# Two norms in one chain, the gain of a norm moved beside its squares, and five changes of order, in a two-part transformer on one core

## The chip, the cores and the metric

One core of one Trainium2 chip runs the whole program in one launch. Time is device microseconds, the median of the runs. The engines are PE (TensorE; PEld is its weight load), DVE (VectorE), ACT (ScalarE), POOL (GpSimd) and SP (SyncE, which issues the weight DMAs here). L12 is line 12 of the kernel.

## The reference, cut to what matters

The model has width 1024 and 256 tokens x; 256 context tokens go beside them. Its first half has two layers of modulated norm, mixing (latent attention, Fourier and a long convolution), modulated norm, and an MLP with squared ReLU; it ends in a norm of x. The second half has a delta-rule layer and a gated linear attention (GLA) layer, each with an MLP, and takes its own context tokens.

```python
def rms_norm(x, g):
    y = x * rsqrt(mean(x * x) + 1e-6)
    return y * g

def modulate(h, shift, scale):
    return h * (1 + scale) + shift

# every norm inside the layers
h = modulate(rms_norm(x, g), shift, scale)
# end of the first half, start of the second
x = rms_norm(x, final_norm_g)
hx = modulate(rms_norm(x, norm_mix_g[0]), shift, scale)
hc = modulate(rms_norm(ctx, norm_mix_g[0]), shift_c, scale_c)
```

## The kernel before

The residual stream X is a tile of 128 partitions by 8 blocks of 128 features by 512 columns: 256 tokens x, then 256 of the context. Stages in which only x matters (the second layer's front, out and mlp, the GLA's out and the last mlp) work on 256 columns. Every product with a weight is three TensorE products in fp32r: high by high, high by rest, rest by high (L558, L559, L560), of which the rest is what the first rounding left. Weights come in slabs of 128 by 2048 through a ring of four, which SP fills in order. For each slab ACT writes w_high and DVE then w_rest. A slab is 48 matmuls.

The stages in order: mod, in0, up0, attention, front, out0, mlp0, norm, in1, up1, attention, front, out1, mlp1, final, conv, delta, read, out of the delta layer, mlp2, norm, gin, gla, out, mlp3. Each engine's instructions are written out by hand in functions named pe_, act_, dve_ and pool_ plus the stage; nothing reorders them. A `View` counts each semaphore through tables of uses (U_IN, U_MLP and so on).

A norm is made like this. In the stage before it, a block of the product is added to X (dve_residual, L1517), ACT squares the block (act_square, L473), DVE adds the squares up (dve_add_square, L479). PE sums over features with a matrix of ones (pe_sums, L493), ACT takes the root (L517), DVE the reciprocal (L521), and PE spreads it over partitions (pe_factors, L501). The head of the next stage then makes h in four steps for each of the eight blocks: dve_scale (X by the factor, L526), act_move (gain and shift, L532), a copy to the high part on ACT, and the rest on DVE:

```python
nc.vector.tensor_tensor(H, X, factors(T), ALU.mult)
nc.scalar.activation(H, H, ACT.Identity, bias=shift, scale=gain)
nc.scalar.activation(high, H, ACT.Copy)
nc.vector.tensor_tensor(rest, H, high, ALU.subtract)
```

At the seam of the halves (dve_final, act_final, pe_final) this is done twice: a norm of x that is written back to X (L1190), then squares, sums and root over X and the context; ACT then issues the DMA that spills X, and the convolution stage begins with a memset (L1813) and its head.

In the up stage queries and keys are made head by head; `weights(2)` makes the parts of the next slab. The delta stage begins with `meet`, at which all engines wait for each other; POOL then makes gates (L2351) and copies keys (L2359) for two units, and PE's first products over keys are L1986. In the GLA recurrence there are 16 units (direction, tile, head). For each, ACT takes exponentials of 128 by 1024 (L2887, two instructions), DVE scales queries by them (L2945), POOL keys (L3029), PE forms pair products in PSUM, and DVE copies eight masked blocks of them to ATG (L2960), of which block n holds pairs that lie in the n-th level of a triangle. PE then forms the outputs.

## Time and profile before

| | |
| --- | --- |
| median of 3 runs | 2904.25 us (2902.1 to 2904.61) |
| the profiled execution | 2905.02 us, its span 2902.9 us |
| PE, PEld busy | 94%, 78% |
| DVE, ACT, POOL busy | 57%, 41%, 13% |
| DMA | 343.36 MB, mean 118 GB/s |

The span runs from the first to the last instruction. The shares are averages over stages with different limits; what a stage waits for is read from its own rows.

### The profile page before, as it was taken

The numbers are of one execution on the slowest core, as the hardware profiler recorded it, in microseconds if no ns is written. First come the engines' busy times: TensorE is split into PE (matmuls) and PEld (weight loads), VectorE is DVE, ScalarE is ACT, GpSimd is POOL, SyncE is SP. The second block draws the span as 40 slices with busy tenths as digits, with TensorE's granted clock in tenths as the row PEclk, the third lists the DMA queues.
The fourth block names the chain that finished last, engine by engine and source line by source line (L and its number), as shares of the span: only waits on it lengthen the run. The fifth ranks groups of instructions, "written<-read, shape, count | busy, mean of one in ns | idle before, by whom it ended". The sixth has DMA issues, their size and how long they took to land.

```text
span 2902.9 us, 43802 instructions
## 1 busy us (share of the span) xinstructions
PE 2729.6 (94%) x16708; PEld 2265.2 (78%) x16708; DVE 1647.1 (57%) x2847; ACT 1177.6 (41%) x2145; POOL 370.2 (13%) x583
## 2 busy tenths in 40 slices
PE   6999899998898997999999999999999998988899
PEld 4756777777757996887688888877777787977899
DVE  4565533334665666885377777773433345468565
ACT  4343422223534445346344455552422234343443
POOL 0000000000000000000066666640000000023000
PEclk9999999999999998999999999999999999999999
DMA  7263244442363553223200000032444433210453
GB/s 281 87 248 130 88 188 159 173 160 86 121 229 132 177 185 144 89 102 109 94 1 1 1 1 1 1 117 87 152 172 170 171 116 127 73 59 15 150 184 144
DMA packets 49614, 343.36 MB, mean 118 GB/s; under 512 B 5296, under 2 KB 7344, under 8 KB 9776
## 3 DMA queue, kind: packets, MB, share of 16 engines
q1 hardware_dynamic: 44960, 324.03, 30.1%
q10 hardware_dynamic: 4496, 17.15, 1.5%
q8 instruction: 108, 1.77, 0.2%
q14 instruction: 50, 0.41, 0.1%
HBM read 333.82 MB, written 7.34 MB: 118 GB/s over the span
## 4 chain that ended last, share of the span: by engine, by line
PE 85%; DVE 8%; ACT 4%; issue 2%; DMA 2%; POOL 0%; DVEq 0%; ACTq 0%; SPq 0%; PEldq 0%; PEld 0%; POOLq 0%
PE ps L558 20%; PE ps L560 20%; PE ps L559 20%; PE ps L2030 4%; PE ps L2017 3%; PE ps L764 3%; PE ps L2009 2%; PE ps L2038 2%; DMA ring<-in_w_dram 2%; PE ps L819 1%; DVE ring_rest L546 1%; ACT H L532 1%; PE ps L1986 1%; PE ps L1972 1%; PE ps L794 1%
## 5 line engine op out<-in xcount | busy, mean ns | idle before, releaser
L558 PE MATMUL ps<-hidden_high,w_high 128*128 128x256 f32 (+1 forms) x1160 | 389.2, 336 | 8.9 <-DVE h_rest L554 6.1
L1130 ACT ACTIVATE w_high<-ring 128x2048 fp32r<-128x2048 f32 x124 | 237.0, 1911 | 381.3 <-DMA ring<-in_w_dram 258.9
L558 PE MATMUL ps<-h_high,w_high 128*128 128x512 f32 (+1 forms) x1024 | 351.2, 343 | 16.4 <-DVE h_low L1553 13.6
L559 PE MATMUL ps<-h_low,w_high 128*128 128x512 f32 (+1 forms) x1024 | 348.0, 340 | 0.0
L559 PE MATMUL ps<-hidden_low,w_high 128*128 128x512 f32 (+1 forms) x1024 | 343.5, 335 | 0.0
L1562 DVE TENSOR_TENSOR mix_high<-ring,w_high 128x2048 fp32r<-128x2048 f32 x56 | 128.4, 2293 | 245.1 <-ACT w_high L1130 245.1
L560 PE MATMUL ps<-hidden_high,ring_rest 128*128 128x256 f32 (+1 forms) x872 | 265.1, 304 | 0.0
L2351 POOL TENSOR_SCALAR RS<-C,arena 128x128 f32<-128x128 f32 x128 | 74.9, 603 | 1444.2 <-DVEq L1932 1444.2
L558 PEld LDWEIGHTS ps<-hidden_high,w_high 128*128 128x128 f32 x1160 | 218.3, 188 | 42.5 <-issue 16.5
L558 PEld LDWEIGHTS ps<-h_high,w_high 128*128 128x128 f32 x1024 | 196.1, 192 | 44.8 <-issue 24.8
L1562 DVE TENSOR_TENSOR ring_rest<-ring,w_high 128x2048 fp32r<-128x2048 f32 x68 | 155.9, 2293 | 123.3 <-ACT w_high L1130 123.3
L559 PEld LDWEIGHTS ps<-h_low,w_high 128*128 128x128 f32 x1024 | 196.4, 192 | 20.4
L559 PEld LDWEIGHTS ps<-hidden_low,w_high 128*128 128x128 f32 x1024 | 192.5, 188 | 19.3
L560 PE MATMUL ps<-hidden_high,mix_high 128*128 128x512 f32 x512 | 199.5, 390 | 0.0
L560 PE MATMUL ps<-h_high,ring_rest 128*128 128x256 f32 (+1 forms) x640 | 199.1, 311 | 0.0
L560 PEld LDWEIGHTS ps<-hidden_high,ring_rest 128*128 128x128 f32 x872 | 168.9, 194 | 7.1
L1517 DVE SCALAR_TENSOR_TENSOR X<-ps,M,X 128x256 f32<-128x256 f32 x240 | 106.0, 479 | 112.0 <-PE ps L560 112.0
L558 PE MATMUL ps<-conv_h_high,conv_w_high 128*128 128x512 f32 (+1 forms) x392 | 156.7, 400 | 7.5 <-DVE h_rest L1822 6.5
L1134 ACT ACTIVATE arena<-ps 128x256 f32<-128x256 f32 (+1 forms) x128 | 62.2, 488 | 246.6 <-PE ps L560 245.3
L560 PE MATMUL ps<-conv_h_high,ring_rest 128*128 128x512 f32 (+1 forms) x392 | 155.4, 396 | 0.0
L559 PE MATMUL ps<-h_rest,conv_w_high 128*128 128x512 f32 (+1 forms) x392 | 154.5, 394 | 0.0
L560 PE MATMUL ps<-h_high,mix_high 128*128 128x512 f32 x384 | 149.6, 390 | 0.0
(445 smaller groups left out, 6112.2 us busy)
## 6 DMA issues: line engine op xcount, KB each, us to landing
ring<-in_w_dram SPq DMA_DIRECT2D x302, 1024.0 KB, 4.8
z_spill<-arena ACTq DMA_DIRECT2D x16, 256.0 KB, 2.0
arena<-z_spill SPq DMA_DIRECT2D x2, 2048.0 KB, 9.6
C<-in_first_dram ACTq DMA_DIRECT2D x1, 2432.0 KB, 12.2
X<-in_x_dram ACTq DMA_DIRECT2D x1, 2048.0 KB, 13.1
x_spill<-X ACTq DMA_DIRECT2D x1, 2048.0 KB, 6.4
X<-x_spill SPq DMA_DIRECT2D x1, 2048.0 KB, 7.6
C<-in_third_dram ACTq DMA_DIRECT2D x1, 2048.0 KB, 10.1
```

The lines of the kernel that those rows point to most:

```text
L558: ins = nc.tensor.matmul(out_, w_high, high, start=first, stop=False)
L559: nc.tensor.matmul(out_, w_high, rest, start=False, stop=False)
L560: return ins, nc.tensor.matmul(out_, w_rest, high, start=False, stop=last)
L764: ins = nc.tensor.matmul(ps[r:r + 32, 6, 0:256], cs(blk, k, n % 4), w[:, k, :], start=(n % 4 == 0 and k < 4), stop=(n % 4 == 3 and k >= 4) ...
L1130: nc.scalar.activation(W_HIGH[:, (j + 1) % 2, :], ring[:, s], ACT.Copy).then_inc(sems["w_high"], 1)
L1134: nc.scalar.activation(RELU[:, n % 2, 0:T], ps[:, b, 0:T], ACT.Relu).then_inc(freed[b], 1)
L1517: ins = nc.vector.scalar_tensor_tensor(X[:, n, s * L:(s + 1) * L], ps[:, b, s * L:(s + 1) * L], M[:, 2 * (gate * KD + n) + s:2 * (gate * K ...
L1562: nc.vector.tensor_tensor(mlp_rest(v, j + 1, own, T), ring[:, v.place(own)], W_HIGH[:, (j + 1) % 2, :].bitcast(F32), ALU.subtract).then_in ...
L2009: ins = nc.tensor.transpose(ps[:, 4 * u, g * P:(g + 1) * P], tt[:, stay * 256 + g * P:stay * 256 + (g + 1) * P], ident[:])
L2017: ins = nc.tensor.matmul(ps[:, 4 * u + 3, g * P:(g + 1) * P], pm_of(u, n)[:, g * P:(g + 1) * P], tt[:, moved * 256 + g * P:moved * 256 + ( ...
L2030: ins = nc.tensor.matmul(ps[:, 4 * u + 1, g * P:(g + 1) * P], unit(u, DT)[:, g * P:(g + 1) * P], unit(u, DT)[:, 256 + g * P:256 + (g + 1) ...
L2351: ins = nc.gpsimd.tensor_scalar(RS[:, u, h * P:(h + 1) * P], cst("incl", d * P, d * P + P), col(SG_, d, c, hp, u, h), None, ALU.mult)
```

## The change

- **Seam.** ACT squares x in mlp1's last quarter times gfw = sqrt(gf² + eps), gf being the final norm's gain; sums, one root and one spread then give the factor of both norms together for x, and of the context's for the rest (eps_second holds a different epsilon for the two). POOL (pool_second) squares and adds the context half, applies its gains, and adds up x² for the final norm alone. Two products with ones, a root and a reciprocal of 256 columns give FACTOR1, with which X is scaled in the convolution's third slab; the spill is issued there.
- **Heads.** In seven of eight stages with a norm (not in0), ACT multiplies a block by its gain beside its square (act_gain), and the head is: factor (DVE), shift and high part (ACT), rest with the shift (DVE).
- **Order.** The up stage of the second layer makes the next slab's parts ahead of its heads. At 256 tokens, w_rest of the out stage's last slab comes after the residuals. In the delta stage POOL makes the first gates before it meets the others, and DVE's memset of SS follows the meeting. In the GLA DVE copies six blocks and ACT three smaller ones (wide_levels) out of levels 6 and 7, and POOL forms seven of eight blocks. In the in stage dve_low is put before dve_filter.

```diff
@@ tiles @@
+eps_second = sb("eps_second", [P, 1])
+gfw = sb("gfw", [P, KD])
...
@@ act_square @@
-def act_square(act, v, n, T):
+def act_square(act, v, n, T, weight=1.0):
     if n >= 3:
         act.wait_ge(sems["added"], v.of("added", n - 2))
-    nc.scalar.activation(square_of(n)[:, 0:T], X[:, n, 0:T], ACT.Square).then_inc(sems["squares"], 1)
+    nc.scalar.activation(square_of(n)[:, 0:T], X[:, n, 0:T], ACT.Square, scale=weight).then_inc(sems["squares"], 1)
...
+def act_gain(act, v, n, T, blk_norm):
+    for s in range(T // L):
+        c = 2 * n + s
+        ins = nc.scalar.activation(H[:, n, s * L:(s + 1) * L], X[:, n, s * L:(s + 1) * L], ACT.Copy, scale=SA[:, blk_norm, c:c + 1])
+    ins.then_inc(sems["h_moved"], 1)
+def dve_factor(dve, v, k, T):
+    dve.wait_ge(sems["h_moved"], v.of("h_moved", k + 1 - KD))
+    if k == 0:
+        dve.wait_ge(sems["spread"], v["spread"])
+    at = quarters(H[:, k, 0:T], T)
+    nc.vector.tensor_tensor(at, at, factors(T), ALU.mult).then_inc(sems["scaled"], 1)
+def shift_of(sh, k, s):
+    at = 2 * (sh + k) + s
+    return M[:, at:at + 1]
+def act_shifted_high(act, v, k, high, T, sh):
+    act.wait_ge(sems["scaled"], v.of("scaled", k + 1))
+    for s in range(T // L):
+        toks = slice(s * L, (s + 1) * L)
+        ins = nc.scalar.activation(high[:, k, toks], H[:, k, toks], ACT.Identity, bias=shift_of(sh, k, s))
+    ins.then_inc(sems["h_high"], 1)
+def dve_shifted_rest(dve, v, k, high, rest, T, sh):
+    dve.wait_ge(sems["h_high"], v.of("h_high", k + 1))
+    for s in range(T // L):
+        toks = slice(s * L, (s + 1) * L)
+        ins = nc.vector.scalar_tensor_tensor(rest[:, k, toks], H[:, k, toks], shift_of(sh, k, s), high[:, k, toks].bitcast(F32), ALU.add, ALU.subtract)
+    ins.then_inc(sems["h_split"], 1)
...
@@ act_mod @@
-            nc.scalar.activation(unread[:], eps32[:], ACT.Sqrt)
+            nc.scalar.activation(gfw[:], vec("gf", 0, KD), ACT.Square).then_inc(act_step, v.step())
+            act.wait_ge(act_step, v.steps())
+            nc.scalar.activation(gfw[:], gfw[:], ACT.Sqrt, bias=eps[:])
...
@@ act_in @@
-        if k < KD:
+        if l == 0 and k < KD:
             act_move(act, v, k, T2, 0, 0)
-        if k > 0:
+        if l == 0 and k > 0:
             act_h_high(act, v, k - 1, HID_HIGH, T2)
+        if l == 1 and k < KD:
+            act_shifted_high(act, v, k, HID_HIGH, T2, 0)
...
@@ act_up, and the same in dve_up @@
-        if h == 4:
+        if h == (0 if l else 4):
...
@@ act_mlp, head @@
-    for k in range(KD + 1):
-        if k < KD:
-            act_move(act, v, k, T, 1, 3 * KD)
-        if k > 0:
-            act.wait_ge(sems["h_moved"], v.of("h_moved", k))
-            nc.scalar.activation(H_HIGH[:, k - 1, 0:T], H[:, k - 1, 0:T], ACT.Copy).then_inc(sems["h_high"], 1)
+    for k in range(KD):
+        act_shifted_high(act, v, k, H_HIGH, T, 3 * KD)
...
@@ act_mlp, last quarter @@
-                act_square(act, v, n, T)
+                act_square(act, v, n, T, 1.0 if host else gfw[:, n:n + 1])
+                if host != (0,) and n == 0:
+                    act.wait_ge(sems["biased"], v.of("biased", 1 if host else 2))
+                if n < KD - 1:
+                    act_gain(act, v, n, T, 0)
...
+S1, S1_LAST = SQR[:, 0, L:T2], SQR[:, 1, L:T2]
+FACTOR1 = RS[:, 1, L:T2]
 def dve_final(dve, v):
-    dve_root(dve, v, 0, 0, L)
-    dve.wait_ge(sems["spread"], v.of("spread", 1))
-    for k in range(KD):
-        nc.vector.scalar_tensor_tensor(quarters(X[:, k, 0:L], L), quarters(X[:, k, 0:L], L), vec("gf", k), factors(L), ALU.mult,
-                                       ALU.mult).then_inc(sems["scaled"], 1)
-    v.go_on(U_FNORM)
+    dve_root(dve, v, 0, 0, T2)
     dve_next_mod(dve, v, 0)
-    for k in range(1, KD - 1):
-        dve_add_square(dve, v, k, T2)
-    dve_root(dve, v, 0, 0, T2)
+    dve.wait_ge(freed[1], v.freed(1, 1))
+    nc.vector.reciprocal(FACTOR1, FACTOR1).then_inc(sems["root"], 1)
...
 def act_final(act, v):
-    act_root(act, v, 0, 0, L)
-    v.go_on(U_FNORM)
+
     act.wait_ge(sems["second_loaded"], 32)
-    for k in range(KD):
-        act.wait_ge(sems["scaled"], v.of("scaled", k + 1))
-        act_square(act, v, k, T2)
-    act_root(act, v, 0, 0, T2)
+    act.wait_ge(filled[0], v.filled(0))
+    nc.scalar.activation(RS[:, 0, 0:P], ps[:, 0, 0:P], ACT.Sqrt, bias=eps_second[:], scale=1024.0 / D).then_inc(freed[0], 1)
+    act_gain(act, v, KD - 1, L, 0)
+    act.wait_ge(filled[1], v.filled(1))
+    nc.scalar.activation(FACTOR1, ps[:, 1, 0:L], ACT.Sqrt, bias=eps[:], scale=1.0 / D).then_inc(freed[1], 1)
...
@@ act_norm @@
     act_root(act, v, 0, 0, T2)
+    act_gain(act, v, KD - 1, T2, 0)
...
 def pe_final(pe, v):
-    pe_sums(pe, v, 0, 0, L, True)
-    pe_factors(pe, v, (0, 0, 0, 0), L)
-    v.go_on(U_FNORM)
-    pe_sums(pe, v, 0, 0, T2)
+    pe.wait_ge(freed[0], v.free(0))
+    pe.wait_ge(sems["added"], v.of("added", 0))
+    pe.wait_ge(sems["squares"], v.of("squares", 0))
+    pe.wait_ge(sems["prod"], v.of("prod", -1))
+    for q in range(4):
+        terms = [RS[:, 0, :], square_of(KD - 1)] if q < 2 else [RS[:, 0, :]]
+        for n, x in enumerate(terms):
+            ins = nc.tensor.matmul(ps[32 * q:32 * q + 32, 0, 0:P], ones[:, 0:32], x[:, q * P:(q + 1) * P], start=(n == 0), stop=(n == len(terms) - 1),
+                                   tile_position=(0, 32 * q))
+    ins.then_inc(filled[0], 1)
     pe_factors(pe, v, (0, 0, 0, 0), T2)
+    pe.wait_ge(freed[1], v.free(1))
+    pe.wait_ge(sems["prod"], v.of("prod", 0))
+    nc.tensor.matmul(ps[:, 1, 0:L], ones[:], S1, start=True, stop=False)
+    nc.tensor.matmul(ps[:, 1, 0:L], ones[:], S1_LAST, start=False, stop=True).then_inc(filled[1], 1)
     v.end(U_SECOND)
...
+def pool_second(pool, v):
+    def add_to(total, k, x, turn):
+        if k > 2:
+            pool.wait_ge(pool_step, v.steps())
+        ins = nc.gpsimd.tensor_tensor(total if k == 0 else turn, x, x, ALU.mult)
+        ins.then_inc(pool_step, v.step())
+        pool.wait_ge(pool_step, v.steps())
+        return nc.gpsimd.tensor_tensor(total, total, turn, ALU.add).then_inc(pool_step, v.step()) if k else ins
+    turns = RELU[:, 0, L:T2], RELU[:, 1, L:T2]
+    pool.wait_ge(sems["second_loaded"], 32)
+    pool.wait_ge(sems["biased"], v.of("biased", 2))
+    for k in range(KD):
+        add_to(RS[:, 0, L:T2], k, X[:, k, L:T2], turns[k % 2])
+    pool.wait_ge(pool_step, v.steps())
+    for k in range(KD):
+        ins = nc.gpsimd.tensor_scalar(H[:, k, L:T2], X[:, k, L:T2], SA[:, 0, 2 * k + 1:2 * k + 2], None, ALU.mult)
+        if k == 0:
+            ins.then_inc(sems["prod"], 1)
+    ins.then_inc(sems["mixed"], 1)
+    for n in range(KD):
+        j = 4 + n // 2
+        b = mlp_bank(j, n % 2, ())
+        pool.wait_ge(freed[b], 3 * mlp_per(b, ()) + v.freed(b, mlp_nth(j, ()) + 1))
+        if n < KD - 1:
+            add_to(S1, n, X[:, n, 0:L], turns[n % 2])
+        else:
+            pool.wait_ge(pool_step, v.steps())
+            nc.gpsimd.tensor_tensor(S1_LAST, X[:, n, 0:L], X[:, n, 0:L], ALU.mult).then_inc(sems["prod"], 1)
+    v.go_on(u_mlp(True))
 def dve_filter(dve, v, l, j):
@@ -1345,12 +1416,15 @@
 def dve_in(dve, v, l):
...
@@ dve_residuals @@
-            dve_w_rest(dve, v, W_HIGH, j)
+            if T == T2 or j < uses["slab"]:
+                dve_w_rest(dve, v, W_HIGH, j)
         for n in (2 * p, 2 * p + 1):
             if n >= 2:
                 dve_add_square(dve, v, n - 1, T)
             dve.wait_ge(filled[n], v.filled(n))
             dve_residual(dve, v, n, n, T, 2)
+    if T == L:
+        dve_w_rest(dve, v, W_HIGH, uses["slab"])
     dve_root(dve, v, 0, 1, T)
...
@@ act_squares @@
             act_square(act, v, n, T)
+            if n < KD - 1:
+                act_gain(act, v, n, T, 1)
     act_root(act, v, 0, 1, T)
+    act_gain(act, v, KD - 1, T, 1)
     v.go_on(uses)
...
@@ dve_mlp @@
     for k in range(KD + 2):
         if k < KD:
-            dve_scale(dve, v, k, T)
+            dve_factor(dve, v, k, T)
         if k > 1:
-            dve.wait_ge(sems["h_high"], v.of("h_high", k - 1))
-            nc.vector.tensor_tensor(H_LOW[:, k - 2, 0:T], H[:, k - 2, 0:T], H_HIGH[:, k - 2, 0:T].bitcast(F32),
-                                    ALU.subtract).then_inc(sems["h_split"], 1)
+            dve_shifted_rest(dve, v, k - 2, H_HIGH, H_LOW, T, 3 * KD)
+    if norm_next and not host:
+        at = VCOL["b_ada"][0] + 16
+        nc.vector.scalar_tensor_tensor(SA[:, 0, :], V[:, at:at + 16], 1.0, vec("gm", 0, 16), ALU.add, ALU.mult).then_inc(sems["biased"], 1)
+        dve.wait_ge(sems["biased"], v.of("biased", 1))
+        of_x = SA[:, 0, :].rearrange("p (k s) -> p k s", s=2)[:, :, 0:1]
+        nc.vector.tensor_tensor(of_x, of_x, vec("gf", 0, KD).rearrange("p (k s) -> p k s", s=1), ALU.mult).then_inc(sems["biased"], 1)
...
@@ act_conv @@
+        if j == 2:
+            act.wait_ge(sems["scaled"], v.of("scaled", KD + 1))
+            act.dma_start(spill, X[:]).then_inc(sems["spilled"], 16)
         if j == 10:
...
@@ dve_conv, head; gin's and in's of the second layer likewise @@
+    dve.wait_ge(sems["mixed"], v.of("mixed", 0))
     for k in range(2):
-        dve_scale(dve, v, k, T2)
+        dve_factor(dve, v, k, T2)
...
@@ dve_conv @@
+        if j == 2:
+            for k in range(KD):
+                ins = nc.vector.scalar_tensor_tensor(X[:, k, 0:L], X[:, k, 0:L], vec("gf", k), FACTOR1, ALU.mult, ALU.mult)
+            ins.then_inc(sems["scaled"], 1)
...
@@ dve_delta @@
+    meet(dve, v)
     nc.vector.memset(SS[:, :, :], 0.0)
-    meet(dve, v)
...
@@ pool_delta @@
-    meet(pool, v)
...
@@ pool_delta @@
+    pool.wait_ge(sems["gates"], v["gates"] - 1)
     for u in range(2):
         gate(0, u)
+    meet(pool, v)
+    for u in range(2):
         keys(0, u)
     for u in range(2):
...
@@ pe_gla @@
+            if i and q:
+                pe.wait_ge(sems["weights"], i)
...
@@ act_gla @@
+    def wide_levels(i):
+        d = gla_unit(i)[0]
+        act.wait_ge(sems["masked"], 2 * i + 2)
+        if i >= 2:
+            act.wait_ge(sems["gla_out"], i - 1)
+        for n, half, first in ((6, 32, 0), (6, 32, 64), (7, 64, 0)):
+            key, query = (first, first + half) if d == 0 else (first + half, first)
+            at = (n - 4) * P + query
+            ins = nc.scalar.activation(ATG[key:key + half, 2 * d + i % 2, query:query + half], ps[key:key + half, 5, at:at + half], ACT.Copy)
+        ins.then_inc(sems["weights"], 1)
...
@@ act_gla @@
     exps(0)
     exps(1)
+    wide_levels(0)
     for i in range(1, 16):
         if i < 15:
             exps(i + 1)
...
@@ dve_gla, weights @@
-        for n in range(8):
+        for n in range(6):
...
@@ pool_gla @@
-        nc.gpsimd.tensor_tensor(KX[i % 2].rearrange("p (n t) -> p n t", t=P), EX[i % 2].rearrange("p (n t) -> p n t", t=P),
-                                spread8(KF, h, t), ALU.mult).then_inc(sems["kx"], 1)
+        nc.gpsimd.tensor_tensor(KX[i % 2].rearrange("p (n t) -> p n t", t=P)[:, 1:8, :], EX[i % 2].rearrange("p (n t) -> p n t", t=P)[:, 1:8, :],
+                                spread8(KF, h, t)[:, 1:8, :], ALU.mult).then_inc(sems["kx"], 1)
...
@@ dve, start @@
+    nc.vector.memset(eps_second[0:64], 1024 * EPS * EPS)
+    nc.vector.memset(eps_second[64:P], 1024 * EPS)
```

## Rows read from the trace of the kernel before

**Rows 1.** The page: busy time by engine; the chain that ended last, by engine.

```profile
PE 2729.6 (94%) x16708; PEld 2265.2 (78%) x16708; DVE 1647.1 (57%) x2847; ACT 1177.6 (41%) x2145; POOL 370.2 (13%) x583
...
PE 85%; DVE 8%; ACT 4%; issue 2%; DMA 2%; POOL 0%; DVEq 0%; ACTq 0%; SPq 0%; PEldq 0%; PEld 0%; POOLq 0%
```

**Rows 2.** Waits of PE: line, releaser, us in total, times, longest.

```profile
PE ps L558 <- DVE h_rest L554: 18.3, 9, 5.2
PE ps L493 <- ACT RS L473: 14.3, 7, 3.3
PE ps L558 <- DVE h_low L1553: 13.6, 4, 4.3
```

**Rows 3.** Timeline at the seam: start us, us, operation, [idle before <- releaser].

```profile
1111.91 1.90 ACT L1130 ACTIVATE w_high<-ring 128x2048 fp32r<-128x2048 f32 x1
...
1122.15 0.48 DVE L1517 SCALAR_TENSOR_TENSOR X<-ps,M,X 128x256 f32<-128x256 f32 x1 [1.43 <-PE ps L560]
...
1125.18 3.22 DVE L1190 SCALAR_TENSOR_TENSOR X<-X,V,ps 128x256 f32<-128x256 f32 x8 [0.57 <-PE ps L501]
...
1137.33 1.36 DVE L1813 MEMSET arena<- 128x1560 f32 x1 [1.34 <-PEq L1250]
...
1154.18 2.29 DVE L546 TENSOR_TENSOR ring_rest<-ring,conv_w_high 128x2048 fp32r<-128x2048 f32 x1 [1.04 <-ACT conv_w_high L541]
```

**Rows 4.** Groups by line and shape: busy us, mean ns | idle before.

```profile
L532 ACT ACTIVATE H<-H,M,SA 128x256 f32<-128x256 f32 x112 | 60.6, 589 | 14.5 <-DVE H L526 14.4
L473 ACT ACTIVATE RS<-X 128x256 f32<-128x256 f32 x15 | 6.2, 418 | 18.4 <-DVE X L1517 18.4
L1748 ACT ACTIVATE arena<-ps 128x64 f32<-128x64 f32 x6 | 0.8, 242 | 0.0
...
L2960 DVE COPY_PREDICATED arena<-C,ps 128x128 f32<-128x128 int32 x128 | 38.5, 300 | 5.4 <-PE ps L2829 0.4
L1869 DVE RECIPROCAL arena<-arena 128x512 f32<-128x512 f32 x4 | 13.4, 3353 | 11.3 <-ACT arena L1757 11.3
L521 DVE RECIPROCAL RS<-RS 128x128 f32<-128x128 f32 x6 | 5.7, 953 | 9.9 <-ACT RS L517 9.9
...
L2383 POOL TENSOR_TENSOR X<-X,RS 128x256 f32<-128x256 f32 x8 | 5.8, 728 | 0.0
```

**Rows 5.** Timeline of PE at mlp0's head.

```profile
334.84 0.77 PE L558 MATMUL ps<-h_high,w_high 128*128 128x512 f32 x1 [4.25 <-DVE h_low L1553]
```

**Rows 6.** Timeline of DVE at the head of the second in stage.

```profile
721.71 1.28 DVE L526 TENSOR_TENSOR H<-X,ps 128x512 f32<-128x512 f32 x2 [1.03 <-PEq L1220]
...
737.33 2.29 DVE L546 TENSOR_TENSOR ring_rest<-ring,hidden_low 128x2048 fp32r<-128x2048 f32 x1 [1.03 <-ACT hidden_low L541]
```

**Rows 7.** Timeline of DVE at mlp1's head.

```profile
933.66 1.08 DVE L526 TENSOR_TENSOR H<-X,ps 128x256 f32<-128x256 f32 x3 [0.83 <-PE ps L501]
...
942.85 2.29 DVE L1562 TENSOR_TENSOR ring_rest<-ring,w_high 128x2048 fp32r<-128x2048 f32 x1 [1.35 <-ACT w_high L1130]
```

**Rows 8.** Timeline of PE in the second up stage.

```profile
806.72 0.69 PE L558 MATMUL ps<-h_rest,hidden_low 128*64 128x512 f32 x1 [5.15 <-DVE ring_rest L1376]
```

**Rows 9.** Timeline at the start of the delta stage.

```profile
1443.80 1.76 DVE L2230 MEMSET arena<- 128x2048 f32 x1 [18.55 <-ACTq L1932]
1445.81 2.34 POOL L2351 TENSOR_SCALAR RS<-C,arena 128x128 f32<-128x128 f32 x4 [1444.21 <-DVEq L1932]
...
1453.07 1.91 PE L1986 MATMUL ps<-X 128*128 128x256 f32 x4
```

**Rows 10.** Timeline of DVE in the GLA recurrence.

```profile
2640.51 3.13 DVE L2945 TENSOR_TENSOR arena<-arena 128x1024 f32<-128x1024 f32 x1
2646.52 1.22 DVE L2945 TENSOR_TENSOR arena<-arena 128x1024 f32<-128x1024 f32 x1
```

**Rows 11.** Windows: us, then busy of PE, PEld, DVE, ACT, POOL; clock, DMA, GB/s.

```profile
806.72:811.88 5.16, 5.16 (x13) 2.74 (x14) 4.86 (x12) 0.59 (x1) 0.00 (x0) 0.51 0.61 203
...
2589.30:2658.70 69.40, 59.38 (x349) 51.29 (x348) 61.68 (x130) 21.96 (x50) 34.91 (x13) 0.94 0.00 1
```

95 lines of the change are left out of this document (43 added, 52 removed).

## The prediction

> **What bounds the kernel now.** I read the page first. PE is busy 94% of the span and carries 85% of the chain that ended last; DVE has 8% of the chain, ACT 4% [rows 1]. So the products themselves set the time, and what a change can win lies in the places where PE stands still. None of PE's instructions for the matrix products is removed here, so the whole gain must come from its waits. The second view is therefore PE's waits in total [rows 2]: the first product of a stage waits for the rest of h (18.3 us in 9 places with L554, 13.6 in 4 with L1553), and the norm's sums wait for the last square (14.3 in 7). Those are the heads and the tails of the norms. Third, the timeline at each place that the diff touches [rows 3, 5, 6, 7, 8, 9]; it gives the order there and what is late next. Last, windows and DVE's rows of the GLA recurrence, which no wait of PE's alone explains [rows 10, 11].
>
> **The change, part by part.** Every gain below is a stretch in which PE idles in the profile and which gets shorter.
>
> *The seam.* From the last residual of the first half (1122.15) to the memset of the next stage (1137.33) lie 15.2 us [rows 3]: eight multiplications of X with the final norm (3.22 us in all), eight squares of 512 columns with six sums, two roots and two spreads. After the change it is one chain behind that residual: the residual 0.48; a square 0.42 [rows 4], 0.5 with the hand-over; strips of sums 0.5; root 0.37, reciprocal 0.95 [rows 4]; spread 0.8. Then two products with S1 (estimate 1.2, twice 0.43 at full clock and 0.85 each at half), a square root over 256 columns (0.46), and the reciprocal of 256 columns. The trace has this for 512 columns (3.35) and for 128 (0.95) [rows 4]: between, 1.75. That is 0.48 + 0.5 + 0.5 + 0.37 + 0.95 + 0.8 + 1.2 + 0.46 + 1.75 = 7.0, and 0.2 for the drain. But the last residual itself comes late: ACT now has gains (about 0.4 each) between w_high (1.90) and the squares, in a loop in which DVE's w_rest waits for ACT and ACT's square for DVE; two or three fall behind the w_high at 1111.91 [rows 3]: 1.6. So the memset moves to 1122.15 + 1.6 + 7.2 = 1131.0, 6.3 earlier. The head behind it: first product at the memset + 6.3 (now 6.05, 1143.38), but the second slab at + 18.6 instead of + 19.1 (1154.18 + 2.29 = 1156.47) [rows 3], 0.5 less at least. What the first half's final norm cost DVE comes back in the convolution's third slab, eight instructions or 3.2 us; DVE is busy there for some 9.5 of each 11.3 us, two slabs are ready ahead, so nothing. If that cover were gone it would cost 3.2. Part: **+6.6** (bounds 5 to 8). The spill's DMA moves from before the convolution to its third slab, past two issues on ACT's queue only; it is awaited at the tenth.
>
> *Heads of the norms.* Today the order is scale (DVE, 0.68), move (ACT, two of 0.59 [rows 4]), copy (ACT, 0.61), rest (DVE, 0.69). The gain leaves the head and goes beside the squares; the move disappears; the rest is formed with the shift in two instructions of 256 columns, which I put at 0.39 each, near L1190's eight in 3.22 (0.40 each, the same form and width [rows 3]); where a source is in PSUM the form takes 0.48 [rows 3]. For the two mlps of 512 tokens (mlp0, mlp2) PE's first wait for the rest, 4.25 us [rows 5], becomes 2.9: +1.3 each, **+2.6**. If DVE's 256-column form takes 0.48, each of DVE's eight steps takes 0.68 + 0.96 = 1.64 against PE's 1.41 and the head gives nothing, or loses a little. For in1 and gin the pace of the head is ACT's and DVE's: second slab's w_rest ends 737.33 + 2.29 = 739.62, which is 17.9 after the spread (721.71) [rows 6]; without the move on ACT (eight chunks, of which DVE's own 0.68 + 0.78 now sets the pace) I get 16.1: +1.8 each, **+3.6**. For the two mlps of 256 tokens: mlp1's second slab is ready 942.85 + 2.29 - 933.66 = 11.5 after the spread [rows 7]; I get 9.9, +1.6, and +2.1 for mlp3.
>
> *Tails at 256 tokens.* w_rest of the last slab (2.29) now comes behind the residuals, not before: last square earlier by 2.29, less the gains on ACT and the reciprocal that now stands behind w_rest: +1.4 in out1, +0.6 in the GLA's out. With the heads: **+3.0** and **+2.7**. w_rest of that slab is needed at the first product of the mlp, which waits for the norm anyway.
>
> *Up stage, second layer.* PE waits 5.15 us for w_rest of the next slab, issued behind four heads [rows 8]; moved ahead of them, it waits for nothing. The dozen products behind it ran at a granted clock of 0.51 and took 5.16 [rows 11]; at full clock that is 5.16 by 0.51 or 2.6 to 2.8, so 2.4 more goes with the wait, if the clock holds. Less 2.1 of new waits, since keys that used to be read out now wait behind it: **+5.4** (4 to 5.5).
>
> *Start of the delta stage.* POOL's four gates take 2.34 us twice [rows 9], and only then its keys; the first product over X comes at 1453.07. All of POOL's work waited for the meeting of engines, and that for DVE, whose memset of SS ends at 1443.80 + 1.76 = 1445.56 [rows 9]. Now the gates come before the meeting and the memset behind it, so the meeting is at 1443.8 at the latest (I take 1443.4, as DVE then has no drain of a write to wait for); PE does its two products over the gates, 1.0 each, and the keys are copied beside them: first product at about 1445.8, **+7.2**. Bound below: if PE waits for the gates of the second group, one 2.34 returns, +4.9. The gates on POOL wait for DVE's last write of the gate table but one; nothing else is queued behind that wait, and nothing waits for SS before the first state.
>
> *GLA.* DVE's eight masked copies of 0.30 [rows 4] become six; POOL's product loses an eighth. 16 units by 2 by 0.30, and the hand-over, is 10.9; POOL's hold, an eighth of about 2.35 or 0.29, by 16 another 4.6; 15.5 at best. But now three copies on ACT (128 by 64 takes 0.24 [rows 4]; I take 0.5 for all three) wait for DVE's last mask of the same unit, and the exponentials of the unit behind the next are queued behind them on ACT. That makes a ring: exponentials 1.08, DVE's scaling of q 1.14, six masked copies with hand-overs 2.0, the wide copies 0.5, the output's copy 0.3 and 0.36 for hand-overs and ACT's other work: 5.38. The trace has 69.4 for thirteen units, 5.34 each [rows 11]. So nothing in the loop, -0.6; the backlog of DVE at the end, 9.15 us behind the last exponentials, falls to 6.1: **+2.4** (bounds -4, if the three copies take 0.73 and a hand-over is added in each of 13 units, and +15.5).
>
> *POOL beside DVE.* The new sums give POOL 37 instructions; the nearest row is 0.73 [rows 4]. 23 of them run in mlp1's first quarter, where a slab of 256 tokens leaves DVE about 0.7 us of slack (estimate). That the two block each other is seen in the GLA: DVE's same instruction took 3.13 us where POOL's was under way and 1.22 where not [rows 10]. 23 by 0.73 is 17 if nothing hides it; they are spread over eight slabs with 0.7 of slack each, 5.6, and only those that meet a DVE instruction count. I take **-2.0**, near the lower end since a slab's three or so cost 2.2 against 0.7 only where they all collide (0 to -17).
>
> *No cost.* The root of gf² in the first stage lies behind the load of X; the two small SA instructions (0.17 each) and the eps memsets are under 0.5 us in all. dve_low ahead of the filter at j = 5 changes nothing, as the filter has nothing there. pe_slab_gemm wasn't called.
>
> **The sum.** 5.4 + 7.2 + 6.6 + 2.6 + 3.6 + 3.0 + 2.7 + 2.4 - 2.0 = 31.5. The profiled execution took 2905.02 (span 2902.9), 0.8 above the median of the runs; against it the changed kernel's comes to 2873.5, and for the median 2904.25 - 31.5 = 2872.8.
>
> **The rivals.** A difference under 0.2% (5.8 us) can't be told from none by these runs.
>
> 1. *The GLA gives all of DVE's saving* (15.5 instead of 2.4): ACT's ring closes well under the 5.34, and DVE's load sets the pace alone. For it: DVE is busy 61.7 of the 69.4 us, more than PE (59.4), so it is the fullest engine there, and ACT is busy 22.0 [rows 11]. Against it: the ring above, which needs no full engine. 2872.8 - 13.1 = 2859.7.
> 2. *POOL blocks DVE throughout mlp1.* All 37 by 0.73 is 27: 2897.8; half of that 2884.3. For it: the 3.13 against 1.22 [rows 10]. Against it: half of DVE's instructions in a slab read PSUM or end before the next is due, and 14 of the 37 run where PE has waits of its own. The Trainium skill (page "SBUF — State Buffer", section "SBUF: two separate sides") has a rule that speaks for this rival: a VectorE instruction with two SBUF inputs and a GpSimd instruction that reads SBUF hold a shared port pair exclusively, whichever came first, and the other waits for all of it. By that rule, the 3.13 agrees, and nothing but the number of collisions limits the loss.
> 3. *The GLA's ring is longer.* POOL takes its turn first in each of 13 units, 3.13 - 1.22 = 1.9 each [rows 10], 24.8 in all: 2897.6. Or the wide copies and their hand-overs take 0.5 more: 6.5, 2879.3.
> 4. *The heads don't pay*: 256-column forms at 0.48. The 6.2 of mlp0, mlp2, in1 and gin is gone: 2879.
> 5. *The other side: PE's clock stays at its lower level through the GLA.* Behind up's wait the granted clock was 0.51 for 5.16 us (1.2 GHz); in the recurrence it is 0.94 with PE busy 59.4 of 69.4 us [rows 11]. If the waits there get longer and the clock stayed at 0.50, 59.4 by 0.94 = 55.8 us of work take 111.6, 42.2 more than the stage: 2872.8 + 42.2 = 2915. It decides from 31.5 / 42.2, three quarters of the stage, on. Against it: PE's waits there don't grow by my sum. The Trainium skill (page "TensorE: Matmul & The Clock Gate", section "Part 1: The HAM clock gate (the "warmup" mystery)") has the clock of this engine follow its activity; by that rule too a stage with more waits can run low throughout, and the 0.51 behind a wait agrees.
>
> **How the numbers follow.** The sum holds in its own range (2863 to 2884): 0.60. Rival 1: 0.11. Rival 2: 0.13. Rival 3: 0.09. Rival 4: 0.03. Rival 5: 0.04. The range of 8 in 10 reaches from close to rival 1 (2859.7), as a mixture of it and the sum, to the half lock of rival 2 with a little for a second shortfall: 2862 to 2886. About 0.10 lies below it (most of rival 1) and 0.10 above it (half of rival 2 and of rival 3's first form, rival 5). Slower by over 0.2% is rival 5, 0.04; within 0.2% is where rivals 2 and 3 meet at their worst, 0.04 of their 0.22; faster is the rest, 0.92.
>
> **What would show it.** The convolution's memset about 7.2 us behind the last residual of the first half (now 15.2); no L1190 at the seam; first delta product 2.4 us behind the meeting; no 5.15 wait in up; thirteen GLA units in about 70 us with `wide_levels` copies of 0.16 each. I'm wrong if w_rest (2.29) in mlp1 rises towards 3 beside POOL's sums, if the head's new STT takes 0.48 and over, if POOL's gates aren't done when DVE meets, or if the GLA's units shrink below 5 us.

## The result, and the profile after

The changed kernel takes 2888.23 us (median of 5 runs, 2886.54 to 2889.86) against 2904.25 (2902.1 to 2905.38): a ratio of 0.9946 (0.9934 to 0.9958), 16.0 us. I had forecast 31.5 us, with 2862 to 2886 as the range. The sign holds, the size is half, and the time lies outside the range. Between the two profiled executions the difference is 2905.02 - 2886.91 = 18.1 us.

The page of the changed kernel, busy time and the chain by engine, against [rows 1]: PE's busy time is the same within 1 us, so the net gain is in its idle time: span less busy is 156.3 us, before 173.3.

```profile
PE 2728.8 (95%) x16684; PEld 2272.9 (79%) x16684; DVE 1634.5 (57%) x2852; ACT 1184.1 (41%) x2218; POOL 412.6 (14%) x620
...
PE 86%; DVE 8%; ACT 3%; issue 2%; DMA 1%; DVEq 0%; ACTq 0%; SPq 0%; POOL 0%
```

PE's waits, against [rows 2] (L569 is the rest with the shift, L478 the square, L484 the sum of the squares, L3067 the masked copies of the GLA):

```profile
PE ps L595 <- DVE h_rest L569: 19.8, 4, 9.1
PE ps L2918 <- DVE arena L3067: 12.1, 8, 2.7
...
PE ps L595 <- DVE h_low L569: 9.4, 4, 3.0
...
PE ps L498 <- ACT RS L478: 9.1, 6, 1.7
...
PE ps L498 <- DVE RS L484: 2.9, 1, 2.9
```

Three rows of the kernel before that belong beside them (L479 the sum of the squares, L2960 the masked copies, L1822 the rest in the convolution's head):

```profile
PE ps L493 <- DVE RS L479: 11.4, 2, 8.4
PE ps L2827 <- DVE arena L2960: 10.5, 6, 2.4
...
PE ps L558 <- DVE h_rest L1822: 6.5, 1, 6.5
```

The waits of the heads and tails fell: for h_rest 18.3 + 6.5 became 19.8, for h_low 13.6 became 9.4, for the sums 14.3 + 11.4 became 9.1 + 2.9. The GLA's wait for masked copies is second now, but it grew only from 10.5 to 12.1, so these totals don't show what the GLA lost. To see where the time went I set the start of every slab's w_high on ACT in one trace against the same one in the other. Their difference is the changed kernel's lead, in us:

| up to | lead before it | lead behind it |
| --- | --- | --- |
| end of the out stage of layer 0 | 0 | 1.7 |
| head of mlp0 | 1.7 | 5.2 |
| second norm and in stage | 5.6 | 8.3 |
| up stage and attention of layer 1 | 8.3 | 13.2 |
| out1 and head of mlp1 | 13.2 | 15.3 |
| mlp1, all but its last slabs | 15.3 | 13.0 |
| its last slabs, with squares and gains | 13.0 | 11.4 |
| the seam | 11.4 | 18.4 |
| delta and its readout | 18.3 | 24.5 |
| out of delta and head of mlp2 | 24.5 | 27.1 |
| gin, its head | 26.8 | 29.4 |
| gin, its slabs | 29.4 | 27.6 |
| **GLA recurrence** | 27.6 | **16.8** |
| out and head of mlp3 | 16.8 | 20.4 |
| mlp3 | 20.4 | 18.0 |

Two things stand out. The GLA, which I had at +2.4, loses 10.9. And both mlps of 256 tokens lose a steady 0.1 us in each slab, as gin's slabs lose 1.8 together.

### The profile page after: what moved, and what is told of

It is laid out like the page before. It is cut to its first block, busy times and chain, and to the rows that moved or that the text cites. A ratio compares the mean times of both kernels' runs of the same rounds, so it can differ in the third digit from the quotient of the medians.

```text
span 2885.1 us, 43897 instructions
## 1 busy us (share of the span) xinstructions
PE 2728.8 (95%) x16684; PEld 2272.9 (79%) x16684; DVE 1634.5 (57%) x2852; ACT 1184.1 (41%) x2218; POOL 412.6 (14%) x620
## 4 chain that ended last, share of the span: by engine, by line
PE 86%; DVE 8%; ACT 3%; issue 2%; DMA 1%; DVEq 0%; ACTq 0%; SPq 0%; POOL 0%
PE ps L595 20%; PE ps L596 20%; PE ps L597 20%; PE ps L2121 4%; PE ps L788 3%; PE ps L2108 3%; PE ps L2100 2%; PE ps L2129 2%; PE ps L843 1%; DVE ring_rest L583 1%; PE ps L818 1%; PE ps L2063 1%; DVE arena L3067 1%; PE ps L2167 1%; PE ps L2077 1%
## 5 line engine op out<-in xcount | busy, mean ns | idle before, releaser
L1655 DVE TENSOR_TENSOR arena<-arena 128x256 f32<-128x256 f32 (+1 forms) x128 | 73.1, 576 | 128.9 <-ACT arena L1159 128.6
```

Of the source, the lines that this page charges most:

```text
L1655: nc.vector.tensor_tensor(SQR[:, n % 2, 0:T], r, r, ALU.mult).then_inc(sems["squared"], 1)
```

## The experiments

**GLA undone.** The change with its GLA put back: 2876.85 us (ratio to before 0.9909, 0.9896 to 0.9923).

```diff
-            wide_levels(0)
...
-                wide_levels(i)
...
-                for n in range(6):
+                for n in range(8):
...
-                pe.wait_ge(sems["weights"], i + 1)
...
-                nc.gpsimd.tensor_tensor(KX[i % 2].rearrange("p (n t) -> p n t", t=P)[:, 1:8, :], EX[i % 2].rearrange("p (n t) -> p n t", t=P)[:, 1:8, :],
-                                        spread8(KF, h, t)[:, 1:8, :], ALU.mult).then_inc(sems["kx"], 1)
+                nc.gpsimd.tensor_tensor(KX[i % 2].rearrange("p (n t) -> p n t", t=P), EX[i % 2].rearrange("p (n t) -> p n t", t=P),
+                                        spread8(KF, h, t), ALU.mult).then_inc(sems["kx"], 1)
```

> The changed kernel with its GLA recurrence put back (eight masked copies on DVE, none on ACT, POOL's product over all eight blocks). Theory (the ring): ACT's copies wait for DVE's last mask, the exponentials queue behind them, so every unit costs a whole ring of 5.34 us plus whatever else ACT has in it; from the exponentials of the third unit to the last the changed kernel took 78.3 us where the one before took 69.4, and to the first part of the out stage's weights it lost 10.9. Put back, the stage is 69 to 70 us again and the kernel 2888.2 - 10.9 = 2877 us (2875 to 2880). Rival (the loss comes from something else that changed place, a clock or a lock from POOL's shape): the time stays within 2 us of 2888.

**GLA alone.** The same lines of the change, and no others, put into the kernel before: 2914.34 us (1.0039, 1.0025 to 1.0052).

> The kernel before with only the GLA part of the change (six masked copies on DVE, three copies on ACT, POOL's product over seven blocks). Theory (the ring): about 10.9 us slower, 2915 (2912 to 2918), the thirteen units in 78 us. Rival (it only loses together with the rest of the change): within 3 us of 2904. My prediction had it 2.4 faster.

Both came as the ring has them: 11.4 us back in the one, 9.7 us lost in the other. It needs nothing of the rest of the change. The windows from the exponentials of the third unit to those of the last, thirteen units, in the changed kernel, then with the GLA undone, then GLA alone (columns as in [rows 11]):

```profile
2561.88:2640.22 78.34, 61.15 (x350) 52.54 (x351) 46.79 (x109) 28.14 (x90) 40.70 (x13) 0.93 0.00 1
```

```profile
2562.12:2631.49 69.37, 58.33 (x350) 50.03 (x349) 62.93 (x134) 22.19 (x50) 33.94 (x13) 0.98 0.00 1
```

```profile
2588.58:2667.62 79.04, 62.61 (x359) 53.62 (x358) 46.70 (x109) 28.29 (x90) 40.73 (x13) 0.91 0.00 1
```

DVE, the fullest engine of the stage before, lost 15 us of work (61.68 in [rows 11], 46.79 now), and the stage got 9 us longer. No engine is full in it: that is what a ring of waits looks like in a window. The timeline shows the ring in one unit (ACT L2991 are the three wide copies, L2980 the exponentials):

```profile
2592.10 1.08 ACT L2980 ACTIVATE arena<-ps 128x512 f32<-128x512 f32 x2
...
2594.42 2.06 DVE L3067 COPY_PREDICATED arena<-C,ps 128x128 f32<-128x128 int32 x6
2596.51 0.62 ACT L2991 ACTIVATE arena<-ps 32x32 f32<-32x32 f32 x3 [3.34 <-DVE arena L3067]
...
2597.44 1.08 ACT L2980 ACTIVATE arena<-ps 128x512 f32<-128x512 f32 x2
2598.62 1.23 DVE L3052 TENSOR_TENSOR arena<-arena 128x1024 f32<-128x1024 f32 x1 [2.14 <-ACT arena L2980]
```

ACT idles 3.34 us for DVE's masks, and then DVE 2.14 for ACT's exponentials, in turn: 2597.44 - 2592.10 = 5.34. My sum gave 5.38 for this. The starts of the exponentials of the thirteen units lie 5.62, 5.68, 5.69, 7.89, 5.34, 5.34, 5.33, 9.24, 6.44, 5.33, 5.30, 5.56 and 5.58 apart: the bare ring in five of them, one more instruction of ACT in five, and the units at the state sums in three. In the kernel before they lie 4.09, 4.31, 6.27, 5.04, 7.46, 3.57, 8.29, 5.32, 5.30, 3.58, 7.69, 3.58 and 4.88 apart. It has three long ones too, but six are under 5, in which the other engines catch up with what the long ones delayed. In the ring none is shorter than 5.3.

**Copies one unit's exponentials later.** ACT still copies, but the exponentials of unit i + 2 stand ahead of the copies of unit i: 2881.59 us (0.9922, 0.9908 to 0.9935).

```diff
+            exps(2)
             wide_levels(0)
             for i in range(1, 16):
-                if i < 15:
-                    exps(i + 1)
+                if i in (4, 8):
+                    act_tail(act, 3 + i // 4)
+                if i < 14:
+                    exps(i + 2)
                 wide_levels(i)
...
-                if i in (4, 8):
-                    act_tail(act, 3 + i // 4)
```

> The changed kernel with ACT still making the three wide copies of a unit, but issued one unit's exponentials later (exponentials of unit i + 2 ahead of the copies of unit i). Theory (the ring closes only since the exponentials are queued behind copies that wait for DVE's masks): the ring opens, most of the 10.9 us comes back, 2873 to 2879. Rival (the copies on ACT are slow as such, or PE's wait for them costs): 2885 to 2888.

6.6 us came back, less than I had expected (9 to 15) and more than the rival. Its window:

```profile
2564.03:2637.09 73.06, 60.52 (x350) 51.85 (x349) 48.38 (x111) 27.83 (x86) 37.55 (x13) 0.95 0.00 1
```

The shortest intervals are now 4.5 instead of 5.3, so the order of the queue closed the ring at 5.3. Two things didn't come back: no interval is as short as the 3.6 of the kernel before, and two at the state sums take 9.2 and 8.5. This order also put act_tail, ACT's part of the state sums, ahead of the exponentials; that it made those two long is argued, not shown.

**Wide copies on DVE.** Three plain copies behind DVE's six masked ones, none on ACT: 2872.92 us (0.9893, 0.9878 to 0.9908).

```diff
-            wide_levels(0)
...
-                wide_levels(i)
...
+                dve.wait_ge(sems["masked"], 2 * i + 2)
+                for n, half, first in ((6, 32, 0), (6, 32, 64), (7, 64, 0)):
+                    key, query = (first, first + half) if d == 0 else (first + half, first)
+                    at = (n - 4) * P + query
+                    ins = nc.vector.tensor_copy(ATG[key:key + half, 2 * d + i % 2, query:query + half], ps[key:key + half, 5, at:at + half])
+                ins.then_inc(sems["weights"], 1)
```

> The changed kernel with the three wide copies made by DVE (plain copies of 32 by 32, 32 by 32 and 64 by 64, right behind its six masked ones) and none on ACT. Theory (the ring through ACT): with the copies off ACT the exponentials run ahead again, so the 10.9 us come back, and DVE saves two masked copies of 0.34 for three of about 0.1: 2877 or a few us less, 2870 to 2877. Rival (six masked copies and narrow copies are themselves the trouble, as PE then waits for both): about 2888.

15.3 us faster than the changed kernel and 3.9 than with the GLA undone. The loss is gone once nothing crosses to ACT. DVE's three copies and its window:

```profile
2564.37 0.61 DVE L3059 COPY arena<-ps 32x32 f32<-32x32 f32 x3
```

```profile
2564.01:2629.07 65.06, 57.32 (x349) 49.45 (x348) 58.26 (x147) 22.19 (x49) 35.81 (x13) 0.97 0.00 1
```

65.06 is 4.3 less than the 69.4 of before [rows 11]. But it isn't the copies that save. DVE's groups in the two windows, first with the GLA undone (masked copies, scaling of q), then here (the same two, and the plain copies):

```profile
L3049 DVE COPY_PREDICATED arena<-C,ps 128x128 f32<-128x128 int32 x104 | 31.2, 300 | 4.5 <-PE ps L2918 0.5
L3034 DVE TENSOR_TENSOR arena<-arena 128x1024 f32<-128x1024 f32 x13 | 23.2, 1784 | 1.9 <-ACT arena L2976 1.9
```

```profile
L3053 DVE COPY_PREDICATED arena<-C,ps 128x128 f32<-128x128 int32 x78 | 23.5, 301 | 3.6 <-PE ps L2920 0.5
L3038 DVE TENSOR_TENSOR arena<-arena 128x1024 f32<-128x1024 f32 x13 | 21.0, 1616 | 2.3 <-ACT arena L2980 2.1
L3059 DVE COPY arena<-ps 32x32 f32<-32x32 f32 (+1 forms) x39 | 7.7, 198 | 0.8
```

31.2 us of copies became 23.5 + 7.7, the same. DVE's busy time fell by 4.7 (62.93 to 58.26), and that lies in the instructions that meet POOL's: the scaling of q 23.2 to 21.0, and the rest of gk 4.1 to 2.0. POOL makes seven blocks for eight here; whether that or the other order of the two engines gave the 3.9 us isn't separated. Of rival 1, DVE's saving in full (15.5), no more than this was had.

**Same place.** The change adds two small tiles, which move every tile behind them by 64 bytes. Here four one-column tiles share one tile, so that the arena is back at its old address: 2885.08 us (0.9935, 0.9922 to 0.9949).

```diff
-        eps = sb("eps", [P, 1])
-        eps32 = sb("eps32", [P, 1])
-        unread = sb("unread", [P, 1])
-        eps_second = sb("eps_second", [P, 1])
+        small = sb("small", [P, 8])
+        eps, eps32, unread, eps_second = (small[:, n:n + 1] for n in range(4))
         gfw = sb("gfw", [P, KD])
+        filler = sb("filler", [P, 8])
```

> The changed kernel with its small tiles packed so that every tile behind them starts at the address of the kernel before (the new tiles had moved them by 64 bytes). Theory (place): in the two MLPs of 256 tokens the products followed each other every 0.1199 us instead of 0.1178 with the granted clock at 1.00 in both, since the operands moved by 64 bytes; at the old place the pitch is 0.118 again, a slab takes 5.65 us instead of 5.76, and with 64 slabs and the smaller stages the kernel gains 5 to 7 us: 2882. Rival (the pitch depends on the program, its fetch or the phase of the engines): pitch and time stay as they are, 2888.

**Before, shifted.** The kernel before with two unused tiles that move the arena by 64 bytes: 2907.96 us (1.0015, 1.0006 to 1.0024).

```diff
         unread = sb("unread", [P, 1])
+        filler = [sb(f"filler{n}", [P, 8]) for n in range(2)]
```

> The kernel before with two unused tiles of 32 bytes in front of the arena, which move everything behind them by 64 bytes, and nothing else. Theory (place): the pitch of the products over 256 columns becomes 0.120 us and the kernel 5 to 7 us slower, about 2910. Rival: no difference, 2904.

The same eight slabs of mlp1 in the kernel before, the changed one, the changed one at the old place, and the one before shifted:

```profile
985.37:1030.74 45.37, 45.37 (x386) 45.30 (x385) 27.70 (x32) 20.61 (x25) 0.00 (x0) 1.00 0.53 185
```

```profile
970.52:1016.61 46.09, 46.09 (x386) 46.09 (x385) 27.77 (x32) 20.58 (x24) 0.00 (x0) 1.00 0.52 182
```

```profile
974.80:1020.18 45.38, 45.38 (x386) 45.31 (x385) 27.69 (x33) 20.61 (x25) 0.00 (x0) 1.00 0.53 185
```

```profile
980.69:1026.78 46.09, 46.09 (x386) 46.09 (x385) 27.77 (x32) 20.60 (x24) 0.00 (x0) 1.00 0.53 182
```

The same products (384 start in each window, and two more reach into it), all back to back, at a granted clock of 1.00 in all four: 45.37 or 46.09, by the place alone. A product over 256 columns follows the last after 0.118 us at one place and 0.120 at the other. The slabs of gin do the same: they keep the lead of 22.2 at the old place and lose 1.8 of it at the new one. Of the whole kernel the place is worth 3.2 and 3.3 us, less than the 5 to 7 that I expected from the pitch. (The runs of the changed kernel, 2886.54 to 2889.86, and of the same at the old place, 2882.39 to 2888.86, overlap; for the kernel before, shifted, the ratio's interval of 1.0006 to 1.0024 is clear of 1.) The traces show where the difference goes. At the start of the out stage of layer 1, the kernel before, shifted, is 5.9 us ahead of the kernel before, and at its end 0.9 behind it; the changed kernel is 5.0 ahead of itself at the old place there. So the new place gains early and loses late. Part of the gain stands at one point: with the arena at its new place the second w_high of the first out stage started at 283.9 to 287.2 us (nine kernels, mean 284.9), at the old one at 286.1 to 288.1 (four, mean 287.0). What lies before it waits in part for weight DMAs; why it comes earlier is open.

**POOL, more of it.** 32 more products of 128 by 256 on POOL in mlp1's first quarter: 2890.59 us (0.9954, 0.9941 to 0.9968), 2.4 more than the changed kernel. The runs overlap (2888.69 to 2891.30, against 2886.54 to 2889.86); at their extremes the difference is 4.8.

```diff
+                for _ in range(2):
+                    nc.gpsimd.tensor_tensor(S1_LAST, X[:, k, L:T2], X[:, k, L:T2], ALU.mult).then_inc(pool_step, v.step())
+                    pool.wait_ge(pool_step, v.steps())
                 add_to(RS[:, 0, L:T2], k, X[:, k, L:T2], turns[k % 2])
```

(and the same ahead of each of the eight gains.)

> The changed kernel with 32 more products of 128 by 256 on POOL in the first quarter of the second MLP (repeats whose result is overwritten). In the trace the lock is seen there: w_rest beside POOL took 2.71 where it takes 2.29 alone, and small DVE instructions 0.95 instead of 0.42, in three slabs, while the chip's lead over the kernel before stayed at 15.2 to 15.6 us. Theory (DVE's slack holds all of it): with 32 more the lock lasts through the whole quarter and costs under 3 us, 2888 to 2891. Rival (POOL's blocking costs PE as I had it, up to 0.73 each): 32 by 0.73 or 23 us more, 2911; half of them 2900.

The two do block each other, as these lines of the changed kernel's DVE show (w_rest, 2.29 where POOL is idle):

```profile
926.48 2.71 DVE L1647 TENSOR_TENSOR ring_rest<-ring,w_high 128x2048 fp32r<-128x2048 f32 x1 [0.90 <-ACT w_high L1155]
...
932.35 2.78 DVE L1647 TENSOR_TENSOR ring_rest<-ring,w_high 128x2048 fp32r<-128x2048 f32 x1 [0.66 <-ACT w_high L1155]
```

and POOL's sum, 0.74 to 0.81 in the rows around it, that ran beside the first of them:

```profile
927.12 2.65 POOL L1301 TENSOR_TENSOR RS<-RS,arena 128x256 f32<-128x256 f32 x1
```

But 32 more of them cost 2.4 us, 0.08 each instead of 0.73, and 0.15 each at the extremes of the runs. In the traces the lead fell by 2.9 us over the fifteen slabs behind mlp1's head with them and by 2.1 without, so only 0.8 was lost where they ran. The reason that fits both lines: who comes second waits for the rest of the other's instruction. POOL's are short, so DVE's long ones lose 0.4 to 0.5, while POOL, which nobody waits for there, loses 2. Beside POOL's gains, which came next, w_rest took 2.29 and 2.33, so the reason doesn't hold for each of POOL's instructions. That DVE's slack in a slab holds most of the loss is argued. The Trainium skill's rule (page "SBUF — State Buffer", section "SBUF: two separate sides") is borne out by the 2.65; the time of PE hangs on which of the two has the short instructions.

**Up stage undone.** The next slab's parts behind four heads again: 2892.64 us (0.9963, 0.9949 to 0.9976).

```diff
-                if h == (0 if l else 4):
+                if h == 4:
```

> The changed kernel with the next slab's parts made behind four heads again in the second up stage. Theory (the step of the sum): PE's 5.15 us wait and the slow clock behind it come back, 5.4 us, 2893.6. Rival (the other engines' backlog eats it by the end of the stage): 2888 to 2890.

4.4 us slower than the changed kernel: the step holds, 1.0 below the forecast, in its bounds of 4 to 5.5. Its one wait of PE for that w_rest is back at 5.0 us.

**Delta start undone.** Memset before the meeting, gates behind it: 2896.37 us (0.9973, 0.9963 to 0.9983), 8.1 slower, a little more than the 6.3 to 7.2 I had expected.

```diff
+            nc.vector.memset(SS[:, :, :], 0.0)
             meet(dve, v)
-            nc.vector.memset(SS[:, :, :], 0.0)
...
+            meet(pool, v)
             for u in range(2):
                 gate(0, u)
-            meet(pool, v)
```

> The changed kernel with the start of the delta stage as before (memset ahead of the meeting, POOL's gates behind it). Theory (the step of the sum): 6.3 to 7.2 us slower, 2894.5 to 2895.4. Rival (the delta recurrence takes the start up in its own waits): 2888 to 2890.

**Tail undone.** w_rest of the out stages' last slab ahead of the residuals again at 256 tokens: 2891.66 us (0.9957, 0.9943 to 0.9971), 3.4 slower.

```diff
-                    if T == T2 or j < uses["slab"]:
-                        dve_w_rest(dve, v, W_HIGH, j)
+                    dve_w_rest(dve, v, W_HIGH, j)
...
-            if T == L:
-                dve_w_rest(dve, v, W_HIGH, uses["slab"])
```

> The changed kernel with w_rest of the out stages' last slab ahead of the residuals again where only 256 tokens are worked on. Theory (the step of the sum, 1.4 and 0.6 net of the gains): w_rest of 2.29 stands before the last residuals in two stages, 2 to 4 us slower, 2890 to 2892. Rival (DVE's order doesn't matter there): 2887.5 to 2889.

**Both repairs.** Wide copies on DVE and the old place: 2868.55 us (0.9872, 0.9857 to 0.9887), the fastest of all, 36 us below the kernel before and 19.7 below the change.

> The changed kernel with both repairs: the three wide copies made by DVE, and the small tiles packed so that the rest lies where it lay in the kernel before. If the two effects add (15.3 and 3.2 us as measured one by one): 2869.7 (2867.5 to 2872). Rival (one hides the other): 2873.

2869.7 was expected if the effects add, 2873 if one hides the other. They add, as far as four runs with a range of 7 us (2864.47 to 2871.48) tell.

## Why the prediction was wrong

**The step that failed: "So nothing in the loop, -0.6" in the GLA's part.** It is a term of +2.4 that measured -9.7 (alone) to -11.4 (undone), 12 to 14 us of the 15.5 by which the sum was off. The ring itself was seen and priced well, 5.38 for 5.34. What was wrong was to set it against the mean of the thirteen units, 5.34. A ring is the shortest that a unit can be; the mean of before was made of long units and short ones of 3.6. I had spread ACT's other work as 0.36 per unit into the ring, and left out that the units with state sums take 7.9 and 9.2 and give nothing back. My bound of -4 for this term came from the copies' length; it should have come from the short intervals: thirteen units at no less than 5.3, plus the excess of the long ones over that (2.6, 3.9 and 1.1 in the trace, and 0.2 to 0.35 in each of five others: 9.0 in all). The trace of the kernel before had enough for this: raise each of its thirteen intervals that is under 5.34 to 5.34, and they grow by 8.4, to 77.8, where 78.34 was measured. Rival 3 named the ring, but made POOL's lock or slow copies lengthen it; neither did. The three copies take 0.62, the interval is the 5.34 of the sum, and DVE's scaling of q took 1.22 us in all thirteen units (POOL's product beside it 3.13, so POOL lost every time). The end of the stage did not gain 3.05 either: from the last exponentials to the next w_high it took 2651.59 - 2640.22 = 11.4, before 9.7.

**Missing altogether: the place of the tiles,** 3.2 us of loss. The part "No cost" doesn't name the two new tiles.

**POOL, -2.0:** the term wasn't measured alone. The price of 0.73 per collision is wrong: at 0.08 us for each of 32 more, the 23 cost about 2, and 3.4 at the extreme of 0.15; rival 2 is ruled out at both of its sizes (27 and 13.5). My sign of being wrong, w_rest rising towards 3 in mlp1, came (2.78) without the loss that it was to announce.

**The seam, +6.6:** the chain behind the last residual took 1118.69 - 1110.81 = 7.9, forecast 7.2; the tail's 1.6 came as forecast (lead 13.0 to 11.4). The lead grew by 7.0 there, so net of the tail 5.4, within 5 to 8. But this trace is one of the better ones. Ten of the kernels here have this seam: the chain took 7.9 in three of them and 8.8 to 9.1 in seven, and in those seven the lead net of the tail was 3.6 to 4.1, below my bound. So the term was too large, by 2.5 to 3 in most of the traces. Timeline of the seam, against [rows 3]:

```profile
1110.81 0.48 DVE L1591 SCALAR_TENSOR_TENSOR X<-ps,M,X 128x256 f32<-128x256 f32 x1 [1.11 <-PE ps L597]
...
1116.38 1.75 DVE L1221 RECIPROCAL RS<-RS 128x256 f32<-128x256 f32 x1 [1.89 <-ACT RS L1235]
1118.69 1.36 DVE L1900 MEMSET arena<- 128x1560 f32 x1 [0.56 <-issue]
...
1124.92 0.76 PE L595 MATMUL ps<-conv_h_high,conv_w_high 128*128 128x512 f32 x1 [9.09 <-DVE h_rest L569]
```

The reciprocal of 256 columns, put between two rows, took the 1.75 taken. The first product is 6.2 behind the memset, forecast 6.3. PE's single wait of 9.09 stands against several of before, 6.5 for the rest and 8.4 for the squares among them. What differs between the traces is the clock. The windows of the eight instructions with S1 (L1285, L1286), here and in the run with the GLA undone:

```profile
1114.70:1115.83 1.13, 1.13 (x8) 0.68 (x4) 0.00 (x0) 0.00 (x0) 0.00 (x0) 1.00 0.00 0
```

```profile
1113.83:1115.88 2.05, 2.05 (x8) 1.14 (x4) 0.00 (x0) 0.00 (x0) 0.00 (x0) 0.52 0.00 0
```

At a granted clock of 1.00 they take 1.13, at 0.52 (the lower level, 1.2 GHz) 2.05; the sum had 1.2 between the two levels. Why the clock had fallen in one and not in the other, with the same work ahead, the runs don't show.

**The heads.** mlp0's first wait is 2.96, forecast 2.9; in1's second slab is ready 729.63 + 2.29 - 715.81 = 16.1 behind the spread, as forecast; mlp1's 926.48 + 2.71 - 919.38 = 9.8, forecast 9.9. The new rest takes 0.48 as a single instruction (0.484 and 0.486 on average), which is rival 4's condition and not the 0.39 I took; but two in a row overlap and take 0.88, 0.44 each, and the heads paid, so rival 4 is out.

```profile
330.08 0.88 DVE L569 SCALAR_TENSOR_TENSOR h_low<-H,M,h_high 128x256 fp32r<-128x256 f32 x2
...
331.10 0.76 PE L595 MATMUL ps<-h_high,w_high 128*128 128x512 f32 x1 [2.96 <-DVE h_low L569]
...
715.81 1.29 DVE L552 TENSOR_TENSOR H<-H,ps 128x512 f32<-128x512 f32 x2 [0.72 <-PEq L1246]
...
729.63 2.29 DVE L583 TENSOR_TENSOR ring_rest<-ring,hidden_low 128x2048 fp32r<-128x2048 f32 x1 [0.40 <-ACT hidden_low L578]
```

PE's first wait fell by 1.3 in mlp0 and in mlp2, as forecast. Yet in this trace the lead grew by 3.5 at mlp0's head. There the first products run at the lower clock, and they did so for less long. The window from the first product to where a product takes 0.40, before and after:

```profile
334.84:341.10 6.26, 6.26 (x15) 4.93 (x16) 5.41 (x9) 6.26 (x14) 0.00 (x0) 0.53 0.47 168
```

```profile
331.10:334.62 3.52, 3.52 (x9) 2.81 (x10) 3.52 (x8) 2.48 (x7) 0.00 (x0) 0.58 0.45 114
```

The clock came back 2.7 us sooner after the first product; that is the rest of the gain. The head alone doesn't set it. The same windows, up to the first product of 0.41 or less, in the run with more of POOL, which has the new head and the same first wait of 2.96, and in the kernel before, shifted, which has the old head:

```profile
330.12:336.23 6.11, 6.11 (x15) 4.81 (x16) 6.11 (x14) 4.10 (x11) 0.00 (x0) 0.50 0.44 174
```

```profile
331.36:335.23 3.87, 3.87 (x10) 3.05 (x11) 3.22 (x6) 3.87 (x9) 0.00 (x0) 0.52 0.37 146
```

By this measure the ten kernels with the new head took from 3.1 to 6.1 us (mean 4.3), the three with the old one 3.9, 5.2 and 6.0 (mean 5.0). So most of this part of mlp0's gain is the luck of a trace. In mlp2 the lead grew by 0.0 to 1.7 over the head in the ten kernels, forecast 1.3. in1 gave 2.7 over its stage and gin 2.6 at its head, where I had 1.8 each; gin's slabs then lost 1.8 by the place of the tiles. The two tails at 256 tokens together are worth the 3.4 of their experiment, more than the 1.4 + 0.6 of the sum.

**Up and delta:** 5.4 forecast, 4.4 measured; 7.2 forecast, 8.1 measured. The start of the delta stage, against [rows 9]: the first product over X stands 1.8 behind POOL's first copy, no longer behind gates. It comes 1453.07 - 1427.12 = 25.95 earlier than before, 7.7 more than the lead of 18.2 ahead of it.

```profile
1425.36 0.80 POOL L2448 COPY X<-arena 128x256 f32<-128x256 f32 x2 [83.33 <-ACTq L2023]
1425.81 1.76 DVE L2322 MEMSET arena<- 128x2048 f32 x1 [18.79 <-ACTq L2023]
...
1427.12 1.03 PE L2077 MATMUL ps<-X 128*128 128x256 f32 x4
```

With the two failed terms at their measured size the sum is 31.5 - 2.4 - 10.5 - 3.2 = 15.4, for 16.0 measured. Of the other terms some were too large (up, seam) and some too small (in1, the start of delta, the tails), and they cancel; that the two figures lie so close is luck, as the seam alone scatters by nearly 2 from trace to trace.
